# Two-block transformer on one core: in the second block's attention, output products are issued ahead of the next unit's transposes

## Chip, cores and metric

The kernel runs on 1 core of one Trainium2 chip, as one program. The time is device microseconds (us) of that core. TensorE does matmuls and transposes, VectorE and ScalarE do the softmax and empty PSUM, SyncE issues the DMAs of the weights.

## What is computed

The reference is a first transformer block stack and a second one behind it, both of depth 2. The change touches only the second one's attention. Cut to that:

```python
def attention(q, k, v, scale):              # in blocks of 128 queries
    s = jnp.einsum('bhgqd,bhkd->bhgqk', qi, k) * scale
    p = jax.nn.softmax(s, axis=-1)
    return jnp.einsum('bhgqk,bhkd->bhgqd', p, v)

# layer 0: context tokens attend to context, latent tokens to context and latent
mix   = token_mix(qg, concat([kg_c, kg]), ..., qm, concat([km_c, km]), ...)
mix_c = token_mix(qg_c, kg_c, vg_c, qm_c, km_c, vm_c, ...)      # not in the last layer
# token_mix: 6 GQA heads (2 kv heads, width 64) and 6 MLA heads (q and k width 96, v width 64),
# merged with a pooling branch and multiplied by w_out
```

There are 256 latent and 256 context tokens, and everything is fp32.

## The kernel before

The second block (`build_second`) runs its two layers one after the other: norm and input projection, per-head norms and rotations, attention, output projection (line 2621), then the MLP with weights split into two fp32r parts. Each engine has its own instruction order, written out by hand, and the engines meet on semaphores.

The attention is cut into **units** of one stream, one head and 128 queries (`units(i)`). Layer 0 has 48 of them: 24 of the context stream, with 256 keys each, then 24 of the latent stream, with 512 keys. Layer 1 has the 24 latent ones. In each stream the heads come as 2 GQA heads, 6 MLA heads, 4 GQA heads, with two units for a head.

A unit passes through these steps, each named by its line:

- TensorE, `scores(n)`: one fp32 product into one of four PSUM banks, line 2510 for GQA (64 rows of the array), line 2512 for MLA (96 rows). The trace shows an fp32 product as two weight loads and two matmuls.
- VectorE, `soft(n)`: maximum of the row (L3036) and its scaling (L3037); then, for the unit before, the reciprocal (L3043) and the normalising of the probabilities (L3044).
- ScalarE, `exponential(n)` (L2787): the exponential, into one of four `prob` buffers.
- TensorE, `turn(n)` (L2581): 2 transposes (context) or 4 (latent) into one of two PSUM banks. It waits for the normalised probabilities (`sm_norm`).
- ScalarE: the copy of the transposed probabilities into one of two `probT` buffers (L2842).
- TensorE, `attend(n)` (L2600): the output product of the unit, 2 (context) or 4 (latent) fp32 products of 64 columns. It waits for that copy (`pt_ready`).
- VectorE, after each fourth unit: a copy of two heads' output into `h` (L3050).

ScalarE's order in its loop is: exponential of unit n, then the copy for unit n-2, which waits for `pt_done` of the same unit. So that copy stands behind an exponential which needs the scores of a unit two later:

```python
            for n in range(2, len(us) + 2):
                if n < len(us):
                    exponential(n)
                ...
                act.wait_ge(*pt_done.at(0, ub + n - 1))
                ...
                go(probT[:, b, 0:nk], ps[2 + b][:, 0:nk], ACT.Copy).then_inc(*pt_ready.up())
```

TensorE's own loop, over the steps n = 2 to number of units + 2, is the one that the change touches: `scores(n)`, `turn(n - 2)`, `attend(n - 3)`. Below, a **step** is one round of that loop.

Of the kernel before, what the change touches and what calls it, by code (L numbers as in the profile page):

```python
# [2074 lines left out]
def build_second(nc, ctx, a, scratch, store, out):  # L2075
# [94 lines left out]
    def cols(s, t=0, n=T):  # L2170
        return slice(s * T + t, s * T + t + n)
# [116 lines left out]
    def tensor_program(pe):  # L2288
# [137 lines left out]
        for i in range(DEPTH):  # L2426
# [66 lines left out]
            def scores(n):  # L2493
                s, hd, t = us[n]
                nk = T if s == CTX else TT
                if n == 0:
                    pe.wait_ge(*mla_std.at(i, 1))
                if n == 1:
                    pe.wait_ge(*mla_dve.at(i, MLA_ROPE_K))
                if n == 2:  # L2500
                    pe.wait_ge(*mla_dve.at(i, mla_keyed(3)))
                if n >= 4:
                    pe.wait_ge(*sm_act.at(0, ub + n - 3))
                bank = ps[SCORE_BANKS[n % 4]]
                q = cols(s, t * P, P)
                if hd < GQ:
                    hi = slice((hd % 2) * HD, (hd % 2 + 1) * HD)
                    same = hd % 2 == hd // (GQ // KVH)
                    key = qk[hi, 3, 0:nk] if same else ksw[hi, 0:nk]
                    last = mm(bank[:, 0:nk], qk[hi, hd // 2, q], key, start=True, stop=True)  # L2510
                else:
                    last = mm(bank[:, 0:nk], qm[0:MQK, hd - GQ, q], km[0:MQK, hd - GQ, 0:nk],  # L2512
                              start=True, stop=True)
                last.then_inc(*sc_done.up())
# [58 lines left out]
            def turn(n):  # L2573
                s, hd, t = us[n]
                if n < 2:
                    pe.wait_ge(*mla_std.at(i, 2 * (MH - 2 + n) + 3))
                pe.wait_ge(*sm_norm.at(0, 2 * (ub + n + 1)))
                if n >= 2:
                    pe.wait_ge(*pt_ready.at(0, ub + n - 1))
                for k in range((T if s == CTX else TT) // P):  # L2580
                    last = nc.tensor.transpose(ps[2 + n % 2][:, k * P:(k + 1) * P],  # L2581
                                               prob[:, n % 4, k * P:(k + 1) * P], ident)
                last.then_inc(*pt_done.up())

            def attend(n):
                s, hd, t = us[n]
                if n == 0:
                    pe.wait_ge(*mla_dve.at(i, mla_keyed(MH - 2)))
                if n == 4:
                    pe.wait_ge(*mla_dve.at(i, MLA_DVE))  # L2590
                pe.wait_ge(*pt_ready.at(0, ub + n + 1))
                pair = n // 4
                if n % 4 == 0 and pair >= 2:
                    pe.wait_ge(*av_out.at(0, ub // 4 + pair - 1))
                hi = slice((hd % 2) * HD, (hd % 2 + 1) * HD)
                nk = (T if s == CTX else TT) // P
                for k in range(nk):
                    kv = hd // (GQ // KVH)
                    v = vg[:, k, kv * HD:(kv + 1) * HD] if hd < GQ else vm[:, k, (hd - GQ) * HD:(hd - GQ + 1) * HD]
                    last = mm(ps[6 + pair % 2][hi, t * P:(t + 1) * P], v, probT[:, n % 2, k * P:(k + 1) * P],  # L2600
                              start=(k == 0), stop=(k == nk - 1))
                last.then_inc(*av_done.up())

            for n in range(2, len(us) + 3):
                if n < len(us):
                    scores(n)
                if n < len(us) + 2:
                    turn(n - 2)
                if n >= 3:
                    attend(n - 3)  # L2610
            pe.wait_ge(*av_out.at(0, (ub + len(us)) // 4))
            lo = 0 if i < DEPTH - 1 else T
            mixed_out = [h[:, k, :] for k in range(KD - 2)] + [pin[:, m, :] for m in range(2)]
# [523 lines left out]
    def mla_keyed(hd):  # L3137

        return MLA_ROOTS + hd + 1
# [66 lines left out]
    @block.tensor  # L3206
    def _(pe):
        tensor_program(pe)
# [43 lines left out]
```

## Time and profile before

| | |
|---|---|
| median of 3 runs (lowest, highest) | 2675.25 us (2674.6, 2683.97) |
| profiled execution, its own time | 2675.32 us |
| its span in the trace | 2673.3 us |
| TensorE matmuls busy | 2602.7 us, 97% |
| weight loads busy | 2309.7 us, 86% |
| VectorE, ScalarE busy | 62%, 38% |
| mean granted TensorE clock | 0.986 |

The profile shows one execution. PE is TensorE's matmul side, PEld its weight loads, DVE is VectorE, ACT is ScalarE. The attention units of the second block run from about 1720 to 1820 us (layer 0) and from about 2386 to 2446 us (layer 1). Busy shares of PE are modelled: matmuls are pipelined, and a short gap between two of them can be hidden in the modelled end of the first, while the row of the weight load shows it.

### The profile page before, as it was taken

To read this page: it belongs to the slowest core of one execution; us is meant where nothing else is said; L and a number is where in the kernel's file an instruction comes from. 1 tells how busy PE (TensorE), PEld (TensorE's weight loads), DVE (VectorE), ACT (ScalarE), POOL (GpSimd) and SP (SyncE) were. 2 spreads that over 40 slices of the span, in tenths; PEclk is the share of its full clock that TensorE was granted. 3 is DMA by queue.
4 is the path that set the end of the run, shared out by engine and by line. 5 is a ranking of instruction groups with operands and counts; after the bars stand their busy time and mean duration, and the time that the engine had idled before them with its cause. 6 is when DMAs were issued, how large, how long until landed. Compare 5 with 4: busy or idle time off the path is not lost. (4 is left out here: it accounts for less than half of the span.)

```text
span 2673.3 us, 44664 instructions
## 1 busy us (share of the span) xinstructions
PE 2602.7 (97%) x18839; PEld 2309.7 (86%) x18839; DVE 1670.5 (62%) x2246; ACT 1004.6 (38%) x1231; POOL 99.2 (4%) x179
## 2 busy tenths in 40 slices
PE   8999988999999999989999999999999999999999
PEld 7999888999999999779999954465899899747999
DVE  6888556778878877656788722462555555354555
ACT  4335401543343354114443321552433333153333
POOL 2110000000101100000001000000000000000000
PEclk9999989999999999999999999999999999999999
DMA  8776300656777765004558752101455655211452
GB/s 283 257 255 198 111 1 19 211 166 223 260 253 240 267 229 162 11 1 146 170 197 267 251 193 75 51 1 48 157 176 175 206 176 182 80 63 48 144 176 91
DMA packets 279510, 415.64 MB, mean 155 GB/s; under 512 B 10105, under 2 KB 235721, under 8 KB 277698
## 3 DMA queue, kind: packets, MB, share of 16 engines
q1 hardware_dynamic: 260332, 348.16, 39.5%
q0 software_dynamic: 18128, 64.20, 6.9%
q8 instruction: 113, 1.85, 0.3%
q10 hardware_dynamic: 902, 1.15, 0.2%
q14 instruction: 35, 0.29, 0.0%
HBM read 399.82 MB, written 13.65 MB: 155 GB/s over the span
## 5 line engine op out<-in xcount | busy, mean ns | idle before, releaser
L627 PE MATMUL ps<-h_high,w_low 128*128 128x256 f32 x2016 | 570.9, 283 | 0.0
L625 PE MATMUL ps<-h_high,w_high 128*128 128x256 f32 x1952 | 557.5, 286 | 7.6 <-DVE h_low L1445 4.7
L627 PEld LDWEIGHTS ps<-h_high,w_low 128*128 128x128 f32 x2016 | 387.4, 192 | 0.0
L625 PEld LDWEIGHTS ps<-h_high,w_high 128*128 128x128 f32 x1952 | 375.2, 192 | 9.7 <-DVE w_low L1463 6.3
L1463 DVE TENSOR_TENSOR w_low<-ring,w_high 128x2048 fp32r<-128x2048 f32 x131 | 299.9, 2290 | 127.3 <-ACT w_high L1181 126.7
L626 PE MATMUL ps<-h_low,w_high 128*128 128x256 f32 x1312 | 371.9, 283 | 0.0
L2915 DVE TENSOR_TENSOR w_low<-ring,w_high 128x2048 fp32r<-128x2048 f32 x96 | 220.0, 2292 | 239.3 <-ACT w_high L2687 239.1
L1181 ACT ACTIVATE w_high<-ring 128x2048 fp32r<-128x2048 f32 x131 | 250.5, 1915 | 261.8 <-DMA ring<-in_ffn_w_in 145.6
L2687 ACT ACTIVATE w_high<-ring 128x2048 fp32r<-128x2048 f32 x96 | 183.8, 1916 | 330.0 <-PE ps L2342 304.2
L626 PEld LDWEIGHTS ps<-h_low,w_high 128*128 128x128 f32 x1312 | 252.6, 193 | 0.0
L1484 DVE SCALAR_TENSOR_TENSOR mod_acc<-wmod,cond,mod_acc 128x512 f32<-128x512 f32 x336 | 230.9, 747 | 0.0
L2340 PE MATMUL ps<-h_high,w_high 128*128 128x256 f32 x768 | 218.3, 284 | 2.8 <-DVE h_low L2884 2.8
L2341 PE MATMUL ps<-h_low,w_high 128*128 128x256 f32 x768 | 217.9, 284 | 0.0
L2342 PE MATMUL ps<-h_high,w_low 128*128 128x256 f32 x768 | 217.9, 284 | 0.0
L2340 PE MATMUL ps<-act_high,w_high 128*128 128x256 f32 x768 | 217.5, 283 | 0.0
L2341 PE MATMUL ps<-act_low,w_high 128*128 128x256 f32 x768 | 217.3, 283 | 0.0
L2342 PE MATMUL ps<-act_high,w_low 128*128 128x256 f32 x768 | 217.3, 283 | 0.0
L625 PE MATMUL ps<-act_high,w_high 128*128 128x256 f32 x704 | 199.8, 284 | 0.0
L626 PE MATMUL ps<-act_low,w_high 128*128 128x256 f32 x704 | 199.2, 283 | 0.0
L627 PE MATMUL ps<-act_high,w_low 128*128 128x256 f32 x704 | 199.2, 283 | 0.0
L1432 DVE TENSOR_TENSOR w_low<-ring,w_high 128x2048 fp32r<-128x2048 f32 x62 | 141.7, 2291 | 74.7 <-ACT w_high L1124 73.9
L2340 PEld LDWEIGHTS ps<-h_high,w_high 128*128 128x128 f32 x768 | 148.1, 193 | 4.0 <-issue 4.0
(440 smaller groups left out, 5333.8 us busy)
## 6 DMA issues: line engine op xcount, KB each, us to landing
ring<-in_w_mlp SPq DMA_DIRECT2D x96, 1024.0 KB, 5.3
ring<-in_ffn_w_in SPq DMA_DIRECT2D x88, 1024.0 KB, 8.7
wmod<-in_w_mod POOLq DMA_DIRECT2D x96, 512.0 KB, 6.4
ring<-in_ffn_w_out SPq DMA_DIRECT2D x44, 1024.0 KB, 5.1
ring<-in_w_mix_in SPq DMA_DIRECT2D x26, 1024.0 KB, 5.5
ring<-in_xattn_w_kv SPq DMA_DIRECT2D x16, 1024.0 KB, 5.5
mod_scratch<-mod_acc POOLq DMA_DIRECT2D x24, 512.0 KB, 5.5
ring<-mod_scratch SPq DMA_DIRECT2D x12, 1024.0 KB, 6.5
```

The costliest lines, as they stand in the source:

```text
L625: mm(dst, w_hi, x_hi, start=start, stop=False, **more)
L626: mm(dst, w_hi, x_lo, start=False, stop=False, **more)
L627: return mm(dst, w_lo, x_hi, start=False, stop=stop, **more)
L1181: go(w_high[buffer], ring[:, tiles.slot(r, b), :], ACT.Copy).then_inc(w_high_ready.sem, 1)
L1432: v.tensor_tensor(w_low[:, n % RING, :], slot(n), w_high[COLUMN_HIGHS[c]], ALU.subtract).then_inc(*column_low.up())
L1463: v.tensor_tensor(w_low[:, slot, :], ring[:, slot, :], w_high[buffer], ALU.subtract).then_inc(w_low_ready.sem, 1)
L1484: v.scalar_tensor_tensor(mod_acc[:, c, :], w, col, mod_acc[:, c, :], ALU.mult, ALU.add).then_inc(mod_step.sem, 1)
L2340: mm(dst, w_hi, x_hi, start=start, stop=False, **more)
L2341: mm(dst, w_hi, x_lo, start=False, stop=False, **more)
L2342: return mm(dst, w_lo, x_hi, start=False, stop=stop, **more)
L2687: go(w_high[parity], ring[:, tiles.slot(r, q), :], ACT.Copy).then_inc(w_high_ready.sem, 1)
L2915: v.tensor_tensor(w_low[:, slot, :], ring[:, slot, :], w_high[parity], ALU.subtract).then_inc(w_low_ready.sem, 1)
```

## The change

In each step of TensorE's loop, the output products of unit n-3 stand in front of the transposes of unit n-2. Nothing else is edited: no engine but TensorE has another order, no semaphore, buffer or size is another.

```diff
             for n in range(2, len(us) + 3):
                 if n < len(us):
                     scores(n)
+                if n >= 3:
+                    attend(n - 3)
                 if n < len(us) + 2:
                     turn(n - 2)
-                if n >= 3:
-                    attend(n - 3)
             pe.wait_ge(*av_out.at(0, (ub + len(us)) // 4))
```

TensorE, in the latent units of MLA heads in layer 0 (`km`, `qm` are keys and queries, `vm` the values, `consts_sb` the identity), before:

```order
L2512 MATMUL ps<-km,qm 128x512 [waits sm2_act]
L2581 MATMUL ps<-consts_sb,prob 128x128 [waits pt2_ready,sm2_norm]
L2581 MATMUL ps<-consts_sb,prob 128x128 x3
L2600 MATMUL ps<-probT,vm 64x128 [waits pt2_ready]
L2600 MATMUL ps<-probT,vm 64x128 x3
L2512 MATMUL ps<-km,qm 128x512 [waits sm2_act]
```

and with the change:

```order
L2512 MATMUL ps<-km,qm 128x512 [waits sm2_act]
L2600 MATMUL ps<-probT,vm 64x128 [waits pt2_ready]
L2600 MATMUL ps<-probT,vm 64x128 x3
L2581 MATMUL ps<-consts_sb,prob 128x128 [waits pt2_ready,sm2_norm]
L2581 MATMUL ps<-consts_sb,prob 128x128 x3
L2512 MATMUL ps<-km,qm 128x512 [waits sm2_act]
```

The group that waits for `pt2_ready` of its own unit (the copy into `probT`) now comes straight behind the scores, and the transposes are what stands ahead of the next scores.

TensorE, at the end of layer 0's attention, behind the last scores (`vg` are GQA values, L2621 the output projection), before:

```order
L2581 MATMUL ps<-consts_sb,prob 128x128 [waits pt2_ready,sm2_norm]
L2581 MATMUL ps<-consts_sb,prob 128x128 x3
L2600 MATMUL ps<-probT,vg 64x128 [waits pt2_ready]
L2600 MATMUL ps<-probT,vg 64x128 x3
L2581 MATMUL ps<-consts_sb,prob 128x128 [waits pt2_ready,sm2_norm]
L2581 MATMUL ps<-consts_sb,prob 128x128 x3
L2600 MATMUL ps<-probT,vg 64x128 [waits pt2_ready]
L2600 MATMUL ps<-probT,vg 64x128 x3
L2600 MATMUL ps<-probT,vg 64x128 [waits pt2_ready]
L2600 MATMUL ps<-probT,vg 64x128 x3
L2621 MATMUL ps<-h_sb,ring 128x512 [waits v_loaded6,av2_out]
```

and with the change:

```order
L2600 MATMUL ps<-probT,vg 64x128 [waits pt2_ready]
L2600 MATMUL ps<-probT,vg 64x128 x3
L2581 MATMUL ps<-consts_sb,prob 128x128 [waits pt2_ready,sm2_norm]
L2581 MATMUL ps<-consts_sb,prob 128x128 x3
L2600 MATMUL ps<-probT,vg 64x128 [waits pt2_ready]
L2600 MATMUL ps<-probT,vg 64x128 x3
L2581 MATMUL ps<-consts_sb,prob 128x128 [waits pt2_ready,sm2_norm]
L2581 MATMUL ps<-consts_sb,prob 128x128 x3
L2600 MATMUL ps<-probT,vg 64x128 [waits pt2_ready]
L2600 MATMUL ps<-probT,vg 64x128 x3
L2621 MATMUL ps<-h_sb,ring 128x512 [waits v_loaded6,av2_out]
```

Before, the last two units' transposes were separated by another unit's product, and their two products stood together at the end. Now transposes, the product of that same unit, transposes, and the product of that same unit alternate, with nothing between a unit's transposes and its product.

## Rows read from the trace of the kernel before

**Rows 1.** Stretches: length, busy time of PE, PEld, DVE, ACT, POOL, then granted clock, DMA.

```profile
1727.96:1743.06 15.10, 14.95 (x81) 9.66 (x80) 11.65 (x44) 9.33 (x31) 0.00 (x0) 1.00 0.00 1
1743.07:1755.67 12.60, 12.60 (x65) 7.23 (x64) 8.81 (x35) 6.95 (x25) 0.00 (x0) 1.00 0.00 1
1764.55:1794.69 30.14, 30.14 (x169) 19.74 (x168) 18.40 (x51) 15.97 (x37) 0.00 (x0) 1.00 0.00 1
1794.69:1813.32 18.63, 18.63 (x100) 10.94 (x99) 10.45 (x30) 9.18 (x23) 0.00 (x0) 1.00 0.00 1
```

**Rows 2.** Waits of 1720 to 1850 us: who waited for whom, total us, times, longest.

```profile
PEld ps L2581 <- DVE prob L3044: 6.1, 14, 0.8
...
PEld ps L2600 <- ACT probT L2842: 2.7, 11, 0.3
```

**Rows 3.** Timeline, context units of a GQA head: start, length, engine, line [idle before].

```profile
1746.09 0.35 DVE L3044 TENSOR_SCALAR prob<-prob,ssum 128x256 f32<-128x256 f32 x1
...
1746.84 0.20 PEld L2581 LDWEIGHTS ps<-consts_sb,prob 128*128 128x128 f32 x2 [0.33 <-DVE prob L3044]
```

**Rows 4.** Timeline, a latent unit of an MLA head.

```profile
1772.09 1.13 PE L2512 MATMUL ps<-km,qm 96*128 96x512 f32 x2
...
1772.63 0.14 PEld L2581 LDWEIGHTS ps<-consts_sb,prob 128*128 128x128 f32 x1 [0.24 <-issue]
1773.05 0.60 PE L2581 MATMUL ps<-consts_sb,prob 128*128 128x128 f32 x4
...
1773.26 0.69 DVE L3036 TENSOR_REDUCE smx<-ps 128x1 f32<-128x512 f32 x1 [0.63 <-PE ps L2512]
...
1774.23 0.78 ACT L2787 ACTIVATE prob<-ps,smx,qroot 128x512 f32<-128x512 f32 x1 [1.16 <-DVE smx L3037]
...
1775.00 0.59 ACT L2842 ACTIVATE probT<-ps 128x512 f32<-128x512 f32 x1
```

**Rows 5.** Timeline, a latent unit of a GQA head.

```profile
1797.36 1.12 PE L2510 MATMUL ps<-qk 64*128 64x512 f32 x2
...
1798.41 0.42 PEld L2581 LDWEIGHTS ps<-consts_sb,prob 128*128 128x128 f32 x4 [0.76 <-issue]
...
1798.52 0.69 DVE L3036 TENSOR_REDUCE smx<-ps 128x1 f32<-128x512 f32 x1 [1.19 <-PE ps L2510]
...
1799.43 0.69 ACT L2787 ACTIVATE prob<-ps,smx 128x512 f32<-128x512 f32 x1 [1.39 <-DVE smx L3037]
```

**Rows 6.** Timeline of the first block, transposes followed by full-width products.

```profile
561.83 0.60 PE L953 MATMUL ps<-consts_sb,prob 128*128 128x128 f32 x4
...
562.16 0.52 PEld L965 LDWEIGHTS ps<-probT,kt 128*128 128x128 f32 x3
```

**Rows 7.** Timeline, a context unit of an MLA head.

```profile
1734.04 0.30 PEld L2512 LDWEIGHTS ps<-km,qm 96*128 96x128 f32 x2 [0.17 <-issue]
...
1734.55 0.37 ACT L2842 ACTIVATE probT<-ps 128x256 f32<-128x256 f32 x1
...
1734.78 0.42 DVE L3036 TENSOR_REDUCE smx<-ps 128x1 f32<-128x256 f32 x1 [0.36 <-PE ps L2512]
1734.97 0.41 PEld L2600 LDWEIGHTS ps<-probT,vm 128*64 128x64 f32 x4 [0.25 <-ACT probT L2842]
...
1735.49 0.56 ACT L2787 ACTIVATE prob<-ps,smx,qroot 128x256 f32<-128x256 f32 x1 [0.56 <-DVE smx L3037]
```

**Rows 8.** Timeline, the last units of layer 0's attention.

```profile
1816.71 0.85 PEld L2600 LDWEIGHTS ps<-probT,vg 128*64 128x64 f32 x8 [0.28 <-ACT probT L2842]
...
1817.72 0.42 PEld L2581 LDWEIGHTS ps<-consts_sb,prob 128*128 128x128 f32 x4 [0.17 <-issue]
...
1818.31 1.72 PEld L2600 LDWEIGHTS ps<-probT,vg 128*64 128x64 f32 x16 [0.17 <-issue]
...
1818.42 0.60 ACT L2842 ACTIVATE probT<-ps 128x512 f32<-128x512 f32 x1 [1.13 <-PE ps L2581]
```

**Rows 9.** Timeline, the first units of layer 1's attention.

```profile
2388.18 0.59 ACT L2842 ACTIVATE probT<-ps 128x512 f32<-128x512 f32 x1
...
2389.90 0.30 PEld L2512 LDWEIGHTS ps<-km,qm 96*128 96x128 f32 x2 [0.17 <-issue]
```

**Rows 10.** Stretches at the start of layer 0's attention, columns as in rows 1.

```profile
1719.80:1723.20 3.40, 2.58 (x11) 1.22 (x11) 2.37 (x7) 2.90 (x7) 0.00 (x0) 0.99 0.77 294
1723.20:1726.60 3.40, 3.40 (x13) 2.12 (x11) 2.00 (x8) 1.57 (x6) 0.00 (x0) 0.51 0.00 0
```

## Prediction, made before the changed kernel ran

> **What bounds the kernel now.** I first cut the attention of layer 0 into stretches of like units [rows 1], to have a period for each kind: 15.10 us for 10 context MLA units, 1.51 us each; 12.60 us for 8 context GQA units, 1.575 each; 30.14 us for 12 latent MLA units, 2.51 each; 18.63 us for 7 latent GQA units, 2.66 each. In three of the four TensorE is busy from end to end; in the context MLA stretch it lacks 0.15 us of 15.10. VectorE and ScalarE have room everywhere. So TensorE's own row of instructions sets the pace, and only what shortens that row, or a wait in it, can pay.
>
> Then I read the waits [rows 2]. They name two: transposes that waited for normalised probabilities, 6.1 us in 14 waits, and products that waited for the copy into `probT`, 2.7 us in 11. The change gives the first of them more time. But the timeline of a waiting unit [rows 3] takes it apart: the normalising ends at 1746.09 + 0.35 = 1746.44, and the weight load that is said to wait for it begins at 1746.84. Other handovers take 0.05 us: in [rows 7] the copy ends at 1734.92 and the load behind it begins at 1734.97. So probabilities had been there for 0.35 us, and the load waited for something of TensorE's own.
>
> [Rows 4, 5] show what. Behind MLA scores (96 rows of the array, 128 columns) the load of the first transpose (128 rows, 128 columns) starts at 1772.63, 0.42 us before its matmul, under the second pass of the scores. Behind GQA scores (64 rows) it starts only at 1798.41, 1.05 us after the scores began against 0.96 us for MLA. A change in the part of the array that is used makes the load wait until the array is empty, about 0.09 us, and then exposes the load itself: 0.05 us before a 128-column matmul (the turn takes 0.59 us in [rows 8], where a product follows, and 4 matmuls with hidden loads 4 x 0.11 + 0.09 = 0.53), and 0.11 us before scores, whose first pass takes 1772.63 - 1772.09 = 0.54 us against 0.42 to 0.43 for the second. So a border costs 0.14 us ahead of products or transposes and 0.20 us ahead of scores.
>
> The Trainium skill, TensorEngine Tiling (Array Packing), section Tiling Modes under Key Properties, says that changing the tiling mode drains TensorE. With that rule, the trace agrees in its 0.09 us.
>
> **The change part by part.** It adds and removes no instruction and no DMA; it moves the products of 72 units past the transposes of the next, on TensorE's queue only. No wait of SP or POOL is passed.
>
> *Borders.* A latent MLA unit has two borders in both orders. Before: transposes to products (0.14), products to scores (0.20). After: scores to products (0.14), products to transposes (0.14), and from transposes to scores no border, because 128 and 96 rows count as the same. No row of the second block shows scores behind transposes of an MLA unit. The nearest rows are [rows 6], where the load for a full-width product starts at 562.16, with the last of the four transposes that began at 561.83 (3 x 0.11 later), so it is hidden; the other end is the 0.20 us of today. I take hidden. TensorE's row for a latent MLA unit then falls from 2.51 to 2.45 us. GQA units have three borders before and after, at the same prices: no change. If every change of mode cost the same, as the skill's sentence might be read, this gain would be nothing: 2 against 2, and the sum below would be 0.9 us higher.
>
> *The wait for the copy.* It now stands straight behind the scores. The chain is: scores n, maximum, exponential n, then the copy for unit n-2 (ScalarE takes it behind that exponential), product n-2, transposes n-1, and scores n+2. It runs over two steps, so half of it is the least period. Latent MLA, by [rows 4]: scores to maximum 1.17, to the exponential 0.97, to the copy 0.77, copy 0.59 and handover 0.05: 3.55 us; product 1.01 and transposes 0.59 [rows 8]; less 0.20 for the border that is gone: 4.95 us, or 2.475 a unit. That is above TensorE's 2.45 and below today's 2.51: gain 0.037 us x 24 units = -0.9 us. Latent GQA, by [rows 5]: the exponential comes 0.91 after the maximum and takes 0.09 less, 3.40 + 1.01 + 0.59 = 5.00, or 2.50, below the 2.66 of TensorE's own row: 0. Context MLA, by [rows 7]: 0.74 to the maximum, 0.71 to the exponential, 0.56 for it, 0.37 + 0.05 for the copy: 2.43; product 0.58 (1734.04 + 1.51 - 1734.97), transposes 0.37 (0.59 less two at 0.11), less 0.20: 3.18, or 1.59 against 1.51: +0.08 x 12 = +1.0 us. Context GQA: 0.15 shorter in the softmax, and its third border stays: 2.28 + 0.58 + 0.37 = 3.23, or 1.615 against 1.575: +0.04 x 12 = +0.5 us. The transposes' wait for probabilities, which the change relaxes by the length of a product, was covered already, so nothing is won there.
>
> *The end of each layer's attention.* Here the cover is gone. In [rows 8] the product at 1816.71 (it waits for a copy behind the last exponential) and the transposes at 1817.72 stay where they are. Today the next products follow at once, at 1818.31, because their copy is done, and the second of the two starts after half of the 1.72 us of loads, about 1819.15. After the change, the next product needs the copy of the transposes just made: the copy starts 0.70 after the transposes begin (1818.42 - 1817.72) and takes 0.60 + 0.05, so the product starts at 1817.72 + 1.35 = 1819.07; the last transposes at 1820.08; the last product at 1821.43. That is 2.3 us later than 1819.15, less 0.06 for its own border counted at 1819.15 as none: +2.2 us. The output projection waits for this product's result, so it is on the path, once in each layer: +4.4 us. The latent stream follows the context stream without a break in layer 0, so there is no third.
>
> *The start.* In layer 1 the first product can start at 2388.18 + 0.59 + 0.05 = 2388.82 [rows 9], transposes follow at 2389.83, scores at 2390.42 less 0.20 = 2390.22, against 2389.90 today: +0.3 us. In layer 0 the second transposes wait for late probabilities in any case; I take 0, with 0.4 to either side.
>
> Sum: -0.9 + 0 + 1.0 + 0.5 + 4.4 + 0.3 = **+5.3 us**, on the profiled execution's 2675.32 us (the median of the runs is 2675.25): **2680.6 us**. About 0.5%, 13.4 us, is what a measurement of this kernel can tell from no change, so this counts as the same.
>
> **Rivals.**
>
> (a) *The clock falls in the new gaps.* In [rows 10] a stretch in which TensorE was busy for 2.58 of 3.40 us was followed by one of 3.40 us at a granted clock of 0.51, the lower of its two levels (1.2 GHz, against 2.4). Each layer's end now has two gaps of some 0.75 us within 4 us, and then the wait for the output copy. For it: about the same idle share as in that row. Against: it did not fall after other short gaps. Price: a stretch of 3.4 us at half speed loses 1.7 us of matmuls, once or in both layers: 2682.3 or 2684.0. [...]
>
> (b) *The border ahead of MLA scores stays.* Transposes are not ordinary products, and the load carries a wait. Then latent MLA is 2.51 + 0.14 = 2.65 a unit (+3.4 in place of -0.9), context MLA (3.18 + 0.20)/2 = 1.69 (+2.2 in place of +1.0), the start 0.2 more: 2686.3. [Rows 6] speak against it.
>
> (c) *The waits for probabilities were real.* The profile's own label says so, and [rows 3] contradict it. Then 6.1 us go, with the end still paid: 2675.3 - 6.1 + 4.4 = 2673.6; 2669.2 if the end is not felt either.
>
> (d) *Slower beyond doubt: the low clock holds in the context MLA units.* TensorE's own work there is 1.43 us a unit (1.51 less the 0.08 by which the 0.25 of [rows 7] exceeds the usual 0.17 in [rows 8]), of 1.59 in future. If the clock fell and stayed down for the 12 units, the 1.07 us of passes in it (2 x 0.21 + 6 x 0.11) would double and make it 2.5: 0.9 x 12 = 11 us more, with the 5.3 of the sum and both stretches of (a) 2695. [...]
>
> That the change does nothing is excluded: the order of instructions shows it in all 72 units.
>
> **How the numbers follow.** Forecast 0.62, which with 0.4 us for the start, 1 us for the context units and the ends' own error spans 2678 to 2683. (a) 0.24, (b) 0.05, (c) 0.05, (d) 0.03, faster than all of these 0.01. The range 2675.0 to 2686.0 takes in the forecast, (a) and most scatter of the runs, and leaves out about 0.14. Faster by over 0.5% has 0.01; slower by over 0.5% has (d) and a little of (a) with (b), 0.04; the rest, 0.95, is within 0.5%.
>
> **What would show it.** Right: latent MLA units 2.47 to 2.48 us apart; latent GQA still 2.66; context MLA near 1.59, with products waiting for ACT `probT` in nearly each, and no wait of transposes; at each end two transposes-to-product gaps of 1.35 us, and the output projection 2.2 us later after the last scores. The loads of MLA scores would begin with the last transpose. Wrong: loads of scores still 0.2 us behind it (b); periods below 1.5 us in the context units (c); a new stretch at clock 0.5 behind 1820 or 2446 us (a).

## The result, and the profile after

| | before | changed |
|---|---|---|
| median of 20 runs (lowest, highest) | 2678.22 us (2674.33, 2683.97) | 2684.45 us (2676.86, 2691.13) |
| ratio, 95% interval | | 1.0025 [1.0018, 1.0032] |
| profiled execution, its own time | 2675.32 us | 2684.51 us |
| span in the trace | 2673.3 us | 2682.5 us |
| TensorE matmuls busy | 2602.7 us | 2605.3 us |
| mean granted clock | 0.986 | 0.983 |

The changed kernel is slower by 0.25%, 6.7 us with an interval of 4.8 to 8.6, against a forecast of 5.3. That is inside the 0.5% that the forecast called the same, and inside its range.

The two traces differ by 9.2 us, but 1.6 us of that lies ahead of the changed code. Executions scatter there although the code ahead is the same: in four traces (before, before_b, before_c and half_old, all described below) the first scores of the second block's attention began at 1707.94, 1717.22, 1712.19 and 1709.76 us. In the first two of these, the earliest and the latest, the mean granted clock ahead of that point was 0.98 and 0.97. So nothing here is read from one trace's total. I cut each trace at the weight loads of the scores and compare stretches of the same units.

The stretches of the changed kernel (length; busy time of PE, PEld, DVE, ACT, POOL; granted clock; DMA). In order: 8 context MLA units up to the first GQA scores, 8 context GQA units, 12 latent MLA units, 7 latent GQA units, and the end of layer 0, from its last scores to the output projection; then the start of layer 1 (its first five scores) and its end.

```profile
1734.36:1747.29 12.93, 11.83 (x67) 7.08 (x66) 9.35 (x35) 7.63 (x25) 0.00 (x0) 1.00 0.01 1
1747.29:1760.20 12.91, 12.89 (x66) 7.24 (x65) 8.62 (x35) 6.74 (x25) 0.00 (x0) 1.00 0.00 1
1769.12:1799.07 29.95, 29.95 (x172) 18.47 (x170) 18.59 (x52) 16.35 (x37) 0.00 (x0) 1.00 0.00 1
1799.07:1817.67 18.60, 18.60 (x99) 10.92 (x98) 10.17 (x31) 9.11 (x22) 0.00 (x0) 1.00 0.00 1
1817.67:1827.42 9.75, 7.18 (x47) 4.94 (x46) 2.78 (x8) 4.85 (x9) 0.00 (x0) 1.00 0.00 2
2378.84:2396.82 17.98, 17.14 (x47) 5.10 (x46) 8.68 (x20) 11.96 (x23) 0.00 (x0) 1.00 0.18 60
2445.43:2455.16 9.73, 7.16 (x47) 4.93 (x46) 2.78 (x8) 4.83 (x9) 0.00 (x0) 1.00 0.00 1
```

Beside them, from the kernel before: the end and the start of layer 1.

```profile
2438.66:2446.13 7.47, 6.91 (x47) 4.97 (x46) 2.90 (x8) 4.91 (x10) 0.00 (x0) 1.00 0.00 1
...
2371.06:2388.66 17.60, 17.46 (x41) 4.42 (x40) 7.70 (x16) 11.93 (x23) 0.00 (x0) 1.00 0.19 61
```

Read together with [rows 1]: the GQA latent units are unmoved (2.66 us each), the MLA latent stretch is 0.2 us shorter, the context GQA stretch 0.3 longer, and both ends are 2.27 us longer (9.74 against 7.47). In the ends TensorE is busy for about the same time as before, 7.16 against 6.91 us; the rest of the 2.27 us is waiting.

The waits of layer 0's attention in the changed kernel (who waited for whom, total us, times, longest):

```profile
PEld ps L2600 <- ACT probT L2842: 30.6, 46, 0.9
...
PEld ps L2581 <- DVE prob L3044: 0.3, 1, 0.3
```

Before, the first stood at 2.7 us in 11 waits, the second at 6.1 us in 14 [rows 2]. These 30.6 us are idle time of the weight loads and not lost time: most of it lies under the passes of the scores. What the wait costs, only the period of a unit tells.

A latent MLA unit of the changed kernel (start, length, engine and line, idle time before):

```profile
1771.20 0.42 PEld L2581 LDWEIGHTS ps<-consts_sb,prob 128*128 128x128 f32 x4 [0.17 <-issue]
...
1771.59 0.30 PEld L2512 LDWEIGHTS ps<-km,qm 96*128 96x128 f32 x2
1771.70 1.02 PE L2512 MATMUL ps<-km,qm 96*128 96x512 f32 x2
...
1772.04 0.59 ACT L2842 ACTIVATE probT<-ps 128x512 f32<-128x512 f32 x1
1772.68 0.85 PEld L2600 LDWEIGHTS ps<-probT,vg 128*64 128x64 f32 x8 [0.78 <-ACT probT L2842]
...
1774.08 0.30 PEld L2512 LDWEIGHTS ps<-km,qm 96*128 96x128 f32 x2
```

Two claims can be read here. The load of the scores at 1771.59 has no idle time before it and stands 0.11 us ahead of its matmul at 1771.70: behind transposes it is hidden, in all 36 MLA units. And the products start at 1772.68, 0.05 us after the copy's end at 1772.63. From scores to scores it is 2.49 us.

The end of layer 1, changed kernel:

```profile
2447.50 0.42 PEld L2581 LDWEIGHTS ps<-consts_sb,prob 128*128 128x128 f32 x4 [0.17 <-issue]
...
2448.84 0.85 PEld L2600 LDWEIGHTS ps<-probT,vg 128*64 128x64 f32 x8 [0.93 <-ACT probT L2842]
...
2449.86 0.42 PEld L2581 LDWEIGHTS ps<-consts_sb,prob 128*128 128x128 f32 x4 [0.17 <-issue]
...
2450.55 0.60 ACT L2842 ACTIVATE probT<-ps 128x512 f32<-128x512 f32 x1 [1.76 <-PE ps L2581]
2451.20 0.85 PEld L2600 LDWEIGHTS ps<-probT,vg 128*64 128x64 f32 x8 [0.93 <-ACT probT L2842]
...
2452.22 0.42 PEld L2581 LDWEIGHTS ps<-consts_sb,prob 128*128 128x128 f32 x4 [0.17 <-issue]
...
2453.56 0.85 PEld L2600 LDWEIGHTS ps<-probT,vg 128*64 128x64 f32 x8 [0.93 <-ACT probT L2842]
...
2455.16 0.30 PEld L2621 LDWEIGHTS ps<-h_sb,ring 128*128 128x128 f32 x2 [0.76 <-DVE h_sb L3050]
```

Three times a product starts 1.34 us after transposes, and each time these are its own unit's, with the copy between them. In the first of the three the copy also stands behind the last exponential, and this product stands as late in the kernel before (3.39 us after the last scores began, against 3.41), so the two others make the difference. In [rows 8] the last two products are one block of 16 matmuls.

### The profile page after: what moved, and what is told of

Read it like the earlier page. It is cut to its first block and busy times, and to the rows that moved or that the text cites. A ratio compares the mean times of both kernels' runs of the same rounds, so it can differ in the third digit from the quotient of the medians.

```text
span 2682.5 us, 44664 instructions
## 1 busy us (share of the span) xinstructions
PE 2605.3 (97%) x18839; PEld 2306.1 (86%) x18839; DVE 1669.3 (62%) x2246; ACT 1004.9 (37%) x1231; POOL 98.9 (4%) x179
```

## The experiments

All are stretches of the second block's attention. Low clock is the time at the lower of the two clock levels that fell into the start and the context MLA stretch; there, only traces with the same low-clock time can be compared. In us, from the traces:

| trace | start, layer 0 | 12 context MLA | low clock in both | 8 context GQA | 12 latent MLA | 7 latent GQA | end 0 | start, layer 1 | end 1 |
|---|---|---|---|---|---|---|---|---|---|
| before | 15.96 | 19.16 | 3.4 | 12.61 | 30.14 | 18.62 | 7.48 | 17.60 | 7.47 |
| before_b | 16.07 | 19.08 | 3.4 | 12.61 | 30.14 | 18.61 | 7.47 | 17.59 | 7.47 |
| before_c | 15.61 | 18.23 | 0 | 12.61 | 30.14 | 18.61 | 7.48 | 17.59 | 7.47 |
| changed | 15.78 | 21.93 | 6.8 | 12.91 | 29.94 | 18.61 | 9.75 | 17.98 | 9.74 |
| again | 15.78 | 21.94 | 6.8 | 12.89 | 29.94 | 18.61 | 9.75 | 17.98 | 9.74 |
| after_c | 16.34 | 20.05 | 3.4 | 12.88 | 29.94 | 18.61 | 9.74 | 17.98 | 9.75 |
| ends_only | 15.61 | 18.24 | 0 | 12.61 | 30.14 | 18.61 | 9.72 | 17.59 | 9.72 |
| steady_only | 16.35 | 20.05 | 3.4 | 12.89 | 29.94 | 18.61 | 7.50 | 17.98 | 7.50 |
| start_old | 16.07 | 19.98 | 3.4 | 12.93 | 29.95 | 18.60 | 9.74 | 17.59 | 9.75 |
| half_old | 16.07 | 19.46 | 3.4 | 12.61 | 30.14 | 18.61 | 7.54 | 17.65 | 7.53 |
| half_new | 15.84 | 22.23 | 6.8 | 13.12 | 30.29 | 18.61 | 9.93 | 19.23 | 9.93 |
| copy_first | 15.11 | 18.18 | 0 | 12.61 | 29.78 | 18.61 | 9.74 | 17.10 | 9.74 |
| copy_first_ends_old | 15.11 | 18.18 | 0 | 12.61 | 29.77 | 18.61 | 7.87 | 17.10 | 7.87 |
| copy_first_latent | 15.57 | 17.50 | 0 | 12.61 | 29.78 | 18.60 | 7.87 | 17.10 | 7.87 |

Outside the two columns with a low clock, repeated kernels agree within 0.03 us. Two columns hold units that are not of their kind: the start of layer 0 has the first 4 context GQA units, and the 4 latent GQA units between the streams are in none (8.88 us before, 8.93 changed).

**The changed kernel again (again).**

> The changed kernel once more, for a second trace. If the +2.6 us of the context stage's extra low-clock time in the first trace came by chance, this run's ends are again +2.27 us each, the context MLA units again 1.59 us apart outside the low stretch, and the low-clock time in the attention of layer 0 differs from the 6.8 us of the first trace. If the change itself makes the clock fall longer, it is 6.8 us there again. Time 1.0015 to 1.003 of the kernel before.

Measured: 1.0020 [1.0008, 1.0032] of the kernel before. Every stretch as in its first trace, the low clock at the start too. So the 6.8 us were not shown to be chance; four runs further down look at that.

**Only the ends (ends_only).** Each of the two splits of the change is one condition:

```diff
-                if n >= 3:
+                ahead = n >= len(us)
+                if ahead and n >= 3:
                     attend(n - 3)
                 if n < len(us) + 2:
                     turn(n - 2)
+                if not ahead and n >= 3:
+                    attend(n - 3)
```

> The new order only in the last three steps of each layer, the old one in all others. Theory (a unit's transposes, copy and product stand bare at the end): both ends 9.74 us from the last scores to the output projection, as in the changed kernel, against 7.47 before, all units before them as before: +4.5 us in all, about 1.0017. Rival (the long ends are the tail of a stall that builds up over the steady units): ends stay at 7.5 us and the time does not move.

Measured: 1.0021 [1.0007, 1.0034]. Its stretches, context MLA, latent MLA and the end of layer 0:

```profile
1728.41:1746.65 18.24, 18.10 (x97) 11.55 (x96) 13.97 (x54) 11.10 (x37) 0.00 (x0) 1.00 0.00 1
1768.14:1798.29 30.15, 30.15 (x170) 19.75 (x169) 18.40 (x51) 15.97 (x37) 0.00 (x0) 1.00 0.00 1
1816.90:1826.61 9.71, 7.16 (x47) 4.93 (x46) 2.90 (x8) 4.79 (x9) 0.00 (x0) 1.00 0.00 2
```

Three steps of each layer carry the whole +2.25 us of its end; all units before them stand as in the kernel before. The rival, a stall that builds up, is out. Twice 2.25 is 4.5 us, as expected, and most of the 6.7.

**All but the ends (steady_only).**

```diff
-                if n >= 3:
+                ahead = n < len(us)
+                if ahead and n >= 3:
```

> The new order in all steps but the last three of each layer. Theory: ends back to 7.5 us each; periods as in the changed kernel: latent MLA 2.48, latent GQA 2.66, context MLA 1.59, context GQA 1.61; in all about +1.3 us, 1.0005. Rival (the steady units cost as much as the ends): more than +3 us.

Measured: 1.0009 [0.9997, 1.0020], with ends of 7.50 us. At the same 3.4 us of low clock as the kernel before, start and context MLA together take 36.40 us against 35.12; context GQA 0.28 more, latent MLA 0.20 and 0.13 less, the start of layer 1 0.38 more: +1.7 us over both layers (188.36 against 186.68, summed over all stretches). The timing says +2.5 us, with an interval from -0.8 to 5.4, which cannot tell 1.7 from the rival's 3; the ends of 7.50 us can. The split adds up: 1.7 + 4.5 = 6.2, and after_c, the whole change at the same low-clock time, has 192.81, +6.1.

**Copy ahead of the exponential (copy_first).** ScalarE's order, on top of the change:

```diff
             for n in range(2, len(us) + 2):
-                if n < len(us):
-                    exponential(n)
                 nk = T if us[n - 2][0] == CTX else TT
...
                 go(probT[:, b, 0:nk], ps[2 + b][:, 0:nk], ACT.Copy).then_inc(*pt_ready.up())
+                if n < len(us):
+                    exponential(n)
```

> The changed kernel, but ScalarE takes the copy of unit n-2 ahead of the exponential of unit n. Theory (the product waits because its copy stands behind an exponential that needs scores of two units later): the wait goes, the one-step chain transposes, copy, product is 1.42 us in context MLA units, so their period falls from 1.59 to about 1.43; context GQA falls from 1.61 to 1.575; latent MLA from 2.48 to 2.455; latent GQA stays at 2.66; ends stay at 9.7 us. Against the changed kernel about -3 us. Rival (the product waits for the copy because its transposes come last in the step before): the periods stay at 1.59 and 2.48 or get longer.

Measured: 1.0005 [0.9993, 1.0016]. Latent MLA units are 2.465 us apart where 2.455 was expected, context GQA 1.575, ends 9.74: as the theory has it. Its attention takes 187.93 us without low clock, against 192.81 in after_c with 3.4 us of it, which is worth about 1.3 us (below): some 3.6 us less, where 3 was expected. The start of layer 1 gains 0.9 us on the changed kernel, which was not expected: the first product there waited for a copy behind an exponential too. Only the context MLA units came out at 1.49, not 1.43. The trace has the reason, a unit of this kernel in the context stream:

```profile
1736.65 0.20 PEld L2581 LDWEIGHTS ps<-consts_sb,prob 128*128 128x128 f32 x2 [0.17 <-issue]
...
1737.12 0.38 ACT L2840 ACTIVATE probT<-ps 128x256 f32<-128x256 f32 x1 [0.56 <-PE ps L2581]
...
1737.56 0.41 PEld L2600 LDWEIGHTS ps<-probT,vm 128*64 128x64 f32 x4 [0.44 <-ACT probT L2840]
...
1738.14 0.20 PEld L2581 LDWEIGHTS ps<-consts_sb,prob 128*128 128x128 f32 x2 [0.17 <-issue]
```

Transposes to copy 0.47, copy and handover 0.44, product 0.58: 1.49 us. I had put the first at 0.42. With the exponential out of the way, this one-step chain is what binds, because in the new order nothing but the scores stands between a unit's transposes and its product. So both theories of this run hold a part: in the changed kernel the two-step chain through the exponential binds (1.59), and the rival's chain lies only 0.1 us under it.

**A dose (half_new, half_old).** Each copy in two halves, in the changed kernel and in the kernel before:

```diff
-                go(probT[:, b, 0:nk], ps[2 + b][:, 0:nk], ACT.Copy).then_inc(*pt_ready.up())
+                go(probT[:, b, 0:nk // 2], ps[2 + b][:, 0:nk // 2], ACT.Copy)
+                go(probT[:, b, nk // 2:nk], ps[2 + b][:, nk // 2:nk], ACT.Copy).then_inc(*pt_ready.up())
```

> A dose: the changed kernel with each copy into probT made in two halves, which lengthens it by some 0.15 to 0.2 us. Theory (half of the two-step chain through the copy sets the period of MLA and context units): context MLA and latent MLA units come 0.08 to 0.1 us further apart (about 1.68 and 2.57), latent GQA stays at 2.66, each end grows by two copies, 0.3 to 0.4 us, to about 10.1. Rival (TensorE's own row sets the latent period): latent MLA stays at 2.48.

> The same dose in the kernel before. Theory: latent units keep 2.51 and 2.66, for there TensorE's own row sets the pace; context MLA grows from 1.51 by less than 0.1 us; the ends stay near 7.5 us, growing by less than 0.3, since a copy lies beside another unit's product. Rival (the copy was as much on the path before): latent units and ends grow as in the other run.

The latent MLA stretch and the end of layer 0, half_new:

```profile
1770.81:1801.10 30.29, 30.21 (x171) 18.46 (x170) 18.54 (x51) 17.04 (x49) 0.00 (x0) 1.00 0.00 1
1819.70:1829.63 9.93, 7.17 (x47) 4.94 (x46) 2.79 (x8) 5.09 (x13) 0.00 (x0) 1.00 0.00 1
```

and half_old:

```profile
1766.78:1796.92 30.14, 30.14 (x169) 19.74 (x168) 18.40 (x51) 16.70 (x49) 0.00 (x0) 1.00 0.00 1
1815.53:1823.07 7.54, 6.91 (x47) 4.97 (x47) 2.90 (x8) 5.09 (x13) 0.00 (x0) 1.00 0.00 1
```

The end of layer 0 in half_new, at its second and third gap:

```profile
1824.20 0.42 PEld L2581 LDWEIGHTS ps<-consts_sb,prob 128*128 128x128 f32 x4 [0.17 <-issue]
...
1824.89 0.38 ACT L2842 ACTIVATE probT<-ps 128x256 f32<-128x256 f32 x1 [1.77 <-PE ps L2581]
1825.17 0.38 ACT L2843 ACTIVATE probT<-ps 128x256 f32<-128x256 f32 x1
1825.60 0.85 PEld L2600 LDWEIGHTS ps<-probT,vg 128*64 128x64 f32 x8 [0.98 <-ACT probT L2843]
```

The dose was smaller than planned: from the first half's start to the second's end it is 0.66 us, 0.06 more than the 0.60 of a whole copy, where I had put down 0.15 to 0.2. The end grows by 0.18 us, which is three such doses and not two: the copy counts in all three gaps. Latent MLA grows by 0.35 us over 12 units in the changed kernel, 0.03 a unit and half of 0.06 as the two-step chain demands, and by 0.00 in the kernel before, whose end grows by 0.06 alone. Latent GQA moves in neither. So before the change the copy was off the path in all latent units, and with it the copy is on the path in the MLA ones. The context units say the same of GQA (+0.21 us for 8 in half_new, 0.00 in half_old), but context MLA grows by 0.30 us over 12 units in both: there the copy was on the path before the change too. (The layer 1 start of half_new held another 3.4 us of low clock and says nothing.)

**Does the new order hold the clock down at the start of layer 0? (before_b, before_c, after_c, start_old)** The kernel before twice, the changed kernel once more, and the changed kernel with the old order in its first six steps of each layer:

```diff
-                if n >= 3:
+                ahead = n >= 8
+                if ahead and n >= 3:
```

> The kernel before, a second trace, for the low-clock time at the start of layer 0's attention (first 16 units). If the new order lengthens it: 0 to 3.4 us here, as in the traces with the old order so far (3.4, 0, 3.4). If it is chance: 6.8 us is as likely here as elsewhere.

> As the run before it: 0 to 3.4 us of low clock in the first 16 units of layer 0 if the order matters, anything up to 6.8 if it is chance.

> The changed kernel, a third trace: 6.8 us of low clock in the first 16 units of layer 0, as in its two traces so far, if the new order's waits at the start hold the clock down; 0 or 3.4 if that was chance. All other stretches as in its first trace within 0.05 us.

> The changed kernel with the old order in the first six steps of each layer. Theory: the start of layer 1 (first scores to the fifth) is back at 17.6 us from 17.98, the low-clock time at the start of layer 0 is 0 to 3.4 us, the ends stay at 9.74 us, periods behind the start 1.59, 1.61, 2.48 and 2.66 as in the changed kernel. Rival (the low clock comes from the steady context units' waits): 6.8 us of low clock, or a low stretch later in the context units.

Low-clock time in the first 16 units of layer 0: with the old order at the start (before, before_b, before_c, half_old, ends_only, start_old) 3.4, 3.4, 0, 3.4, 0, 3.4 us; with the new one (changed, again, after_c, half_new, steady_only) 6.8, 6.8, 3.4, 6.8, 3.4; with the copy first (three traces, two of them with the new order at the start) 0 each. after_c missed its 6.8, start_old came as expected, and its start of layer 1 is back at 17.59. The lean is clear, the count small: by the means (2.3 and 5.4 us) the new order comes with some 3 us more of low clock there, and where its waits are gone (copy first) with none. What that costs can be read between traces of one kernel, start and context MLA together: 37.71 us with 6.8 us of low clock against 36.39 with 3.4, 1.3 us; before and before_c, 35.12 against 33.84 with none, give the same. It stays open as a cause: runs enough to settle it were not made. It does not show in the mean clock of the timed runs: 0.9836 over the 12 of this kernel made with "again", 0.9828 over the 35 of the kernel before beside them; the scatter of the first block may hide it.

**Two versions meant to beat the kernel before (copy_first_ends_old, copy_first_latent).** Both copy first. The first has TensorE's new order in all steps but the last three (`ahead = n < len(us)`), the second only in steps with scores of latent units:

```diff
-                if n >= 3:
+                ahead = n < len(us) and us[n][0] == LAT
+                if ahead and n >= 3:
```

> Copy ahead of the exponential, TensorE in the new order in all steps but the last three of each layer. Context MLA units 1.49 us apart as in the run with the copy first, latent MLA 2.46, ends 7.5 us each: about -1.7 us against the kernel before. If the long ends came from ScalarE's order and not from TensorE's, they would stay at 9.7 us.

> A version meant to beat both: ScalarE copies before it takes the exponential; TensorE has the new order only in the steps that issue scores of latent units, the old one in the context units and in the last three steps. From the theory: context MLA units 1.43 us apart (no wait left), context GQA 1.575, latent MLA 2.46, latent GQA 2.66, ends 7.5 us each. Against the kernel before: -1.0 in context MLA, -0.7 in latent MLA, -0.5 at the start of layer 1, about -2.2 us in all, 0.999, which timing can barely tell; the trace can. Rival (the old order needs the exponential first): context MLA units stay at 1.51 or get longer.

Measured: 0.9980 [0.9968, 0.9992] and 0.9998 [0.9987, 1.0009]. By the stretches the second should be the better one: its attention takes 183.98 us against 184.19, and 185.38 for before_c, all without low clock in the context units. So they save 1.2 us (1.7 expected) and 1.4 us (2.2 expected) there, 0.05%. The rest of the first one's 0.2% is not in its stretches. The mean clock of its runs, 0.9847 against 0.9827 of the kernel before, points to scatter outside the changed code; that is argued and not shown. The context MLA units of the second (8 of them), and its end:

```profile
1731.69:1743.19 11.50, 11.50 (x66) 7.28 (x65) 9.11 (x35) 8.31 (x24) 0.00 (x0) 1.00 0.01 1
...
1812.87:1820.74 7.87, 6.98 (x47) 4.97 (x47) 2.79 (x8) 5.39 (x9) 0.00 (x0) 1.00 0.01 2
```

1.44 us a unit with TensorE busy throughout: the 0.08 us of wait that [rows 7] show are gone, and with them the last thing that ScalarE cost TensorE in that stretch. Its ends take 7.87, not the expected 7.5. The trace shows why:

```profile
1816.13 0.68 ACT L2790 ACTIVATE prob<-ps,smx 128x512 f32<-128x512 f32 x1
...
1817.13 0.49 DVE L3047 TENSOR_SCALAR prob<-prob,ssum 128x512 f32<-128x512 f32 x1
1817.67 0.42 PEld L2581 LDWEIGHTS ps<-consts_sb,prob 128*128 128x128 f32 x4 [0.54 <-DVE prob L3047]
```

The last exponential now stands behind a copy, so the last unit's probabilities are normalised only at 1817.62, and its transposes start 0.05 us later. The product ahead of them had begun at 1816.28; in steady_only, where the exponential comes first, the last transposes follow the same product after 1.02 us, here after 1.39. So the copy first has a price where the last unit's probabilities are waited for: 0.37 us in each layer.

## Why the prediction was right

**The bound.** Right. TensorE's own row sets the pace of the latent units: GQA kept 2.66 us through every reordering and dose. (The products of 70 units pass other transposes, not of 72: each layer's last product has none behind it.)

**The waits of [rows 2] are a misreading by label.** Right. Relaxing the wait for probabilities by the length of a product won nothing anywhere, rival (c) with its -6.1 us is out: the 8 context GQA units, where 8 of the 14 labelled waits stood (2.7 of the 6.1 us), became longer (12.61 to 12.91 us), and so did the 4 latent GQA units between the streams, with 4 more of them (3.0 us; 8.88 to 8.93). One of those four, in the kernel before:

```profile
1758.73 0.20 PEld L2581 LDWEIGHTS ps<-consts_sb,prob 128*128 128x128 f32 x2 [0.76 <-DVE prob L3044]
```

The same 0.76 us of idle time stands in [rows 5] with the label `issue`: it is the rest of the scores and the border, whatever the label says.

**The borders.** Right in kind, a little large in size. The load of MLA scores hides behind transposes; rival (b) is out. With the copy's wait removed (copy_first), the latent MLA stretch shows TensorE's own row bare: 29.78 us, 0.36 less than 30.14, with units 2.465 us apart instead of 2.45. The border's price is seen in the scores themselves: their two passes take 1.13 us behind products [rows 4] and 1.02 behind transposes (the trace at 1771.70). The Trainium skill's sentence, TensorEngine Tiling (Array Packing), section Tiling Modes, Key Properties, holds in the traces of the kernel before and the changed one: at each change from transposes or products at full clock the next load that waited for no other engine started 0.20 us after the last matmul had started, and between transposes and MLA scores, in either order, together with it. Read as one price for each change, it would have given no gain, and the measurement decides against that reading: both orders have two borders in a unit, and it takes 2.465 us against 2.51.

**Latent MLA, -0.9 us.** The mechanism was right, the term too large: -0.20 and -0.14, in all -0.34. The period is 2.47 and 2.49 in turn, near the forecast 2.475 (in layer 1 one interval takes 2.55). But I multiplied by 24, and in each layer one of the 12 intervals is the one ahead of the first GQA scores, 2.69 us. There the transposes are followed by scores that use 64 rows of the array, and the 0.20 us border comes back. The gain is on the steps whose next scores are MLA, 11 in a stretch of 12, less what is paid on leaving it.

**Context units, +1.0 and +0.5 us.** Right. Context MLA intervals outside the low clock alternate between 1.52 and 1.66, 1.59 on average; GQA 1.61. Without the low clock's part (after_c against before, 3.4 us each) start and MLA are +1.27 us together and 8 GQA units +0.27. The context MLA part holds the same missed border: its last interval, ahead of GQA scores, takes 1.72 us (1.76 in after_c) against 1.49. The start of layer 0, taken as 0, is 15.78 us without low clock against 15.61.

**The ends, +4.4 us.** Right: 2.27 in each layer, 4.5 together, and ends_only isolates it. The start of layer 1: +0.3 forecast, +0.38 measured.

**Rivals (a) and (d), the clock.** (a) was wrong in its place: in none of the seven traces with the long ends did the clock fall there, through 2.6 us of idle time in 9.7 us. The clock did lean at the other end, at layer 0's start, where TensorE had been waiting already [rows 10]; I had priced that start at nothing, and the means above put the clock's share there at about 1.2 us. The price was high as well: 3.4 us of low clock cost 1.3 us there, where I had put 1.7. Of (d), what came is a part: in two of the changed kernel's three traces 6.8 us of low clock lay in the context MLA units, but then the clock was back at 1.00, through a stretch in which TensorE was busy for 11.83 of 12.93 us.

Terms as measured: 1.27 (start and context MLA), 0.27 (8 context GQA units; the other 4 are in the start), 0.05 (the units between the streams), -0.34, 4.5, 0.38: 6.1 us, which is also after_c less before, 192.81 less 186.68, at the same low-clock time. With the clock's lean it is 7.3; the timing says 6.7, within 4.8 to 8.6. Of the 0.8 us between 6.1 and the forecast's 5.3, the latent MLA term makes 0.6.

## What to carry to other kernels

In a software pipeline written out by hand, two groups that are independent in the steady state are not so at the end: order them there so that each hand-over still has another unit's work beside it. Moving a consumer forward pays only if its producer chain, through every engine and behind whatever stands ahead of it in their queues, has that much slack; half of a two-step chain is the number to compare with the period. And a label on a wait does not give its cost: compare when the named work ended with when the waiting load began.

## What the runs showed that I had not expected

- In copy_first, a transposes-to-copy hand-over took 0.47 us with two transposes, against an estimate of 0.42, which moved a period from 1.43 to 1.49.
- Splitting a PSUM copy of 128x512 on ScalarE into two halves of 128x256 added only 0.06 us to its chain (0.66 against 0.60 us): the second starts 0.28 us after the first, which takes 0.38, so they overlap.
- With the copy first, the ends take 7.87 us and not 7.5: the last transposes then wait for probabilities, and there the label names the cause.
- The time ahead of the changed code differed by up to 9.3 us between executions of the same kernel (1707.94 and 1717.22), while 12 latent MLA units took 30.14 us in every trace of the old order.
